# Attention probabilities and values as float32r parts with three products, values one token tile behind, the last heads under the next panel

## The chip, the cores and the metric

The kernel is one launch on one core of a Trainium2 chip. The metric is the device time of the launch in microseconds. Before the change it is 1859.57 us, the median of three runs (1858.75 to 1859.9).

## The reference, cut to what matters

Two transformer blocks over 512 tokens of width 1024, all in float32. Each has a windowed attention with 16 query heads of width 64 on 4 key and value heads. A block of 128 queries sees the key blocks beside it: three in the first block (before, own, after), two in the second (before, own), fewer at the ends of the sequence.

```
# first block (window_attention)
logits = jnp.where(valid, q @ k * 64 ** -0.5 + bias, -inf)
m = jnp.maximum(jnp.max(logits, -1), sink)
p = jnp.exp(logits - m)
p = p / (jnp.sum(p, -1) + jnp.exp(sink - m))
out = jnp.einsum('bngrqk,bnkgd->bnqgrd', p, vb)
# second block (swa_mixer): the same with ALiBi for a bias, divided after the product
o = jnp.einsum('bkgts,bskd->btkgd', p, vb) / denom
```

Around them stand projections, a state space branch, gates, norms and MLPs.

## The kernel before

Weights arrive as 66 panels of 1024 x 512, in eight steps (k) of 128 rows. For exact enough products in the float32r type, each operand is kept as a rounded part and a rest (`w_hi`, `w_lo`, `a_hi`, `a_lo`), and every product is three float32r matmuls: hi x hi, hi x lo, lo x hi. `main_step` does one step k of a panel: for each of four tiles m it waits, at k = 0, until DVE or ACT has freed that bank (`bank_free`), runs `before(m)`, then the three matmuls of 512 columns (L300), then `after(m)`. ACT rounds the weights (L259), GpSimd takes the rest (L263).

The attentions stand in four stretches of eight heads: `att1` (first block) and `att2` (second block), each for j = 0 and 1. In each, `query_panel` makes the queries (L1800 is its second half); then `heads` runs the next panel, one head behind another under its eight steps. Under step t, per token tile m: TensorE turns the probabilities of head t-1 (`pe_turn_p`, L789, 128x128 transposes into one PSUM bank, 2), the three panel matmuls, the values of head t-1 (`pe_values`, L802, float32, one product per key tile, into bank 3), the logits of head t+1 (`pe_logits`, L772 and L773, banks 0 and 1 in turn). A token tile has 2, 3, 3, 2 key tiles in `att1` and 1, 2, 2, 2 in `att2`. ACT copies the turned probabilities to SBUF (`act_turned`, L880) and takes the exponentials (`act_exp`, L850, from `lg` into `pr`); DVE adds bias and minimum to the logits (`dve_logits`, L819), sums and inverts the denominators (`dve_den`, L889, L891) and multiplies the output (`dve_out`, L897). `pe_values` of tile 0 waits for `dve_out` of the head before, as there is one values bank.

At the end of a stretch `att1` does head 7 on its own, after the panel. `att2` does it under the first step of the next panel (`last_head`). In both, DVE takes the panel's four banks one after another (L2162 with the gate bias, L2280 as a copy) and then does the denominators and output of head 7. In `att2` the gates (L2285, L2287) follow, and TensorE turns the gated outputs (L372) for the next operand.

The order on each engine is the program's order, written out by hand; semaphores tie the engines together. PE's loop over the heads before:

```
def before(m):
    if t: att.pe_turn_p(pe, j, t - 1, m)
def after(m):
    if t: att.pe_values(pe, j, t - 1, m)
    if t < 7: att.pe_logits(pe, j, t + 1, m, og)
main_step(pe, p + 1, t, h, l, False, og + 1, before=before, after=after)
```

## Time and profile before

| | us |
|---|---|
| median of three runs | 1859.57 |
| profiled execution | 1861.01 |
| its span | 1859.1 |
| TensorE matmul busy | 1810.3 (97%) |
| DVE busy | 832.6 (45%) |
| ACT busy | 848.2 (46%) |

The span is from the first to the last instruction of the profiled execution; its own time has 1.9 us around it. Times of rows are microseconds from the span's start, PE is a matmul on TensorE and PEld a weight load, which may run beside a matmul. A matmul's duration includes its way through the array, so what it costs in a queue is the distance between starts. L and a number is the line of the code; the name left of the arrow is written, those right of it are read. What stands in brackets behind an instruction is the idle time of its engine before it and what ended it. TensorE's granted clock is full in the stretches of the attentions.

### The profile page before, as it was taken

To read this page: it belongs to the slowest core of one execution; us is meant where nothing else is said; L and a number is where in the kernel's file an instruction comes from. 1 tells how busy PE (TensorE), PEld (TensorE's weight loads), DVE (VectorE), ACT (ScalarE), POOL (GpSimd) and SP (SyncE) were. 2 spreads that over 40 slices of the span, in tenths; PEclk is the share of its full clock that TensorE was granted. 3 is DMA by queue.
4 is the path that set the end of the run, shared out by engine and by line. 5 is a ranking of instruction groups with operands and counts; after the bars stand their busy time and mean duration, and the time that the engine had idled before them with its cause. 6 is when DMAs were issued, how large, how long until landed. Compare 5 with 4: busy or idle time off the path is not lost.

```text
span 1859.1 us, 26998 instructions
## 1 busy us (share of the span) xinstructions
PE 1810.3 (97%) x9064; PEld 1505.4 (81%) x9064; DVE 832.6 (45%) x1384; ACT 848.2 (46%) x1795; POOL 834.8 (45%) x598
## 2 busy tenths in 40 slices
PE   8999999999999999999999999999999999999998
PEld 7788888887888888888888888877888888887776
DVE  4688888888304443235430033050253311534644
ACT  4655555554325655324442244253533332456652
POOL 4654555577353132435444444445454444442322
PEclk9999999999999999999999999999999999999999
DMA  5732121222133121423233333324232223221211
GB/s 175 138 90 69 56 68 56 60 64 57 57 102 120 52 79 51 132 89 102 83 98 102 91 102 91 102 81 159 81 108 80 85 86 102 80 71 57 63 40 57
DMA packets 46223, 159.85 MB, mean 86 GB/s; under 512 B 4763, under 2 KB 7195, under 8 KB 45884
## 3 DMA queue, kind: packets, MB, share of 16 engines
q1 hardware_dynamic: 38592, 140.53, 24.7%
q10 hardware_dynamic: 7548, 18.20, 4.0%
q8 instruction: 54, 0.88, 0.2%
q14 instruction: 29, 0.24, 0.0%
HBM read 152.42 MB, written 6.29 MB: 85 GB/s over the span
## 4 chain that ended last, share of the span: by engine, by line
PE 81%; DVE 8%; issue 4%; ACT 4%; POOL 1%; DMA 1%; DVEq 0%; ACTq 0%; POOLq 0%
PE main L300 60%; PE main L328 4%; PE aux L802 4%; PE aux L656 2%; PE main L1800 2%; PE aux L789 2%; DVE u_acc L2002 1%; PE aux L772 1%; PE aux L372 1%; DVE x_res L564 1%; PE aux L773 1%; DVE y_all L2080 1%; PE aux L1888 1%; PE aux L647 1%; ACT w_hi L259 1%
## 5 line engine op out<-in xcount | busy, mean ns | idle before, releaser
L263 POOL TENSOR_TENSOR w_lo<-raw,w_hi 128x512 fp32r<-128x512 f32 x504 | 700.7, 1397 | 895.0 <-ACT w_hi L259 883.1
L259 ACT ACTIVATE w_hi<-raw 128x512 fp32r<-128x512 f32 x486 | 304.5, 630 | 696.7 <-PE main L300 683.7
L300 PE MATMUL main<-w_hi,a_hi 128*128 128x512 f32 x736 | 304.2, 413 | 2.3 <-ACT vv L1547 1.5
L300 PE MATMUL main<-w_hi,a_lo 128*128 128x512 f32 x736 | 288.1, 391 | 0.0
L300 PE MATMUL main<-w_lo,a_hi 128*128 128x512 f32 x736 | 287.3, 390 | 0.0
L300 PE MATMUL main<-a_hi,w_hi 128*128 128x512 f32 x576 | 231.2, 401 | 1.6 <-ACT u_raw L1296 1.6
L300 PE MATMUL main<-a_hi,w_lo 128*128 128x512 f32 x576 | 225.2, 391 | 0.0
L300 PE MATMUL main<-a_lo,w_hi 128*128 128x512 f32 x576 | 224.9, 390 | 0.0
L300 PEld LDWEIGHTS main<-w_hi,a_lo 128*128 128x128 f32 x736 | 138.1, 188 | 30.3
L300 PEld LDWEIGHTS main<-w_hi,a_hi 128*128 128x128 f32 x736 | 138.5, 188 | 28.4 <-ACT vv L1547 1.9
L300 PEld LDWEIGHTS main<-w_lo,a_hi 128*128 128x128 f32 x736 | 138.8, 189 | 23.0
L300 PE MATMUL main<-w_hi,f_hi 128*128 128x512 f32 x352 | 138.6, 394 | 1.5 <-DVE f_lo L385 1.5
L300 PE MATMUL main<-w_hi,f_lo 128*128 128x512 f32 x352 | 137.2, 390 | 0.0
L300 PE MATMUL main<-w_lo,f_hi 128*128 128x512 f32 x352 | 137.1, 389 | 0.0
L300 PEld LDWEIGHTS main<-a_hi,w_hi 128*128 128x128 f32 x576 | 108.5, 188 | 25.0 <-issue 2.8
L300 PEld LDWEIGHTS main<-a_hi,w_lo 128*128 128x128 f32 x576 | 108.4, 188 | 23.7
L300 PEld LDWEIGHTS main<-a_lo,w_hi 128*128 128x128 f32 x576 | 108.6, 188 | 22.3
L2002 DVE SCALAR_TENSOR_TENSOR u_acc<-u_raw,par,u_acc 128x510 f32<-128x510 f32 (+1 forms) x128 | 112.3, 946 | 2.4 <-DVE hst L2059 2.3
L802 PEld LDWEIGHTS aux<-v_sb,pt 128*128 128x128 f32 x544 | 70.3, 190 | 39.5 <-ACT pt L880 22.1
L802 PE MATMUL aux<-v_sb,pt 128*128 (+1 forms) x544 | 83.0, 278 | 4.5 <-ACT pt L880 2.9
L880 ACT ACTIVATE pt<-aux 128x256 f32<-128x256 f32 (+2 forms) x128 | 50.7, 397 | 75.5 <-PE aux L789 73.1
L300 PEld LDWEIGHTS main<-w_hi,f_hi 128*128 128x128 f32 x352 | 66.1, 188 | 15.1 <-DVE f_lo L385 1.8
(320 smaller groups left out, 3111.7 us busy)
## 6 DMA issues: line engine op xcount, KB each, us to landing
raw<-w_stream_in SPq DMA_DIRECT2D x264, 512.0 KB, 3.6
x_res<-x_in ACTq DMA_DIRECT2D x8, 512.0 KB, 5.1
rel_rows<-rel_row ACTq DMA_DIRECT2D x1, 4096.0 KB, 44.3
bias<-rel_rows ACTq DMA_DIRECT2D x2, 1536.0 KB, 8.3
out<-x_res SPq DMA_DIRECT2D x4, 512.0 KB, 2.7
bgate<-b_gate_in ACTq DMA_DIRECT2D x4, 256.0 KB, 5.8
ln_g<-ln_g_in ACTq DMA_DIRECT2D x1, 1024.0 KB, 4.7
ln_b<-ln_b_in ACTq DMA_DIRECT2D x1, 1024.0 KB, 6.8
```

The source lines that it names most:

```text
L259: eng.activation(w_hi[:, k, :], raw[:, k, :], ACT.Copy).then_inc(hi_done, 1)
L263: eng.tensor_tensor(w_lo[:, k, :], raw[:, k, :], w_hi[:, k, :].bitcast(F32), ALU.subtract).then_inc(lo_done, 1)
L300: mm = eng.matmul(mb[m][:, :], lhs, rhs, start=(first and k == 0 and n == 0), stop=(last and k == KT - 1 and n == 2))
L328: mm = eng.matmul(out, lhs, rhs, start=(first and k == 0 and n == 0), stop=(last and k == KT - 1 and n == 2))
L372: t = eng.transpose(b[:, m * P:m * P + P], self.src[:, m, c:c + P], ident)
L564: eng.scalar_tensor_tensor(x_res[:, m, :], self.fb[:, m, :], small[:, self.s + m:self.s + m + 1], x_res[:, m, :], ALU.mult, ALU.add).then_ ...
L656: x = eng.matmul(ab[c // 2][:, (c % 2) * GW + r * HP:(c % 2) * GW + r * HP + HP], dmat[r][:, dr, c * P:c * P + P], xdt[:, dr, c, r * HP:r ...
L789: x = eng.transpose(self.turned_bank(t, c)[:, b * P:b * P + P], self.pr[t % 2][:, c, off + b * P:off + b * P + P], ident)
L802: x = eng.matmul(ab[3][:, c * HP:c * HP + HP], pt[c % 2][:, b * P:b * P + P], v_sb[:, lo + b, bass.ds(j * P + half * HP, HP)], start=(b == ...
L880: eng.activation(pt[c % 2][:, 0:nb * P], self.turned_bank(t, c)[:, 0:nb * P], ACT.Copy).then_inc(p_in, 1)
L1800: mm = pe.matmul(mb[m][:, :], lhs, rhs, start=False, stop=(k == KT - 1 and n == 2))
L2002: ins = dve.scalar_tensor_tensor(acc, u_raw[:, m, i0:i0 + o1_ - o0], tap(m, k), acc, ALU.mult, ALU.add)
```

## The change

- Values: the turned value vectors go to `v_hl` as a rounded part (ACT) and a rest (DVE, new `dve_v`).
- Probabilities: ACT's copy of the turned probabilities becomes the rounded part `p_hi`; DVE subtracts it from the bank into `p_lo` (`dve_rest`, new). `pe_values` does three float32r products per key tile in place of one float32 product, with a wait for `p_rest` ahead of the last ones.
- The exponentials are written over the logits (`lg`), `pr` is gone. The four new tiles `pt` take its room.
- Turned probabilities use banks 1 and 2 in turn, logits bank 0 alone from the second head on.
- `pe_values` of a token tile comes one tile later; that of tile 3 under tile 0 of the next step. `dve_out` of a head comes one head later.
- Head 7 of both attentions runs under the first step (and the first tile of the second) of the next panel. DVE's taking of the four banks is now interleaved with `dve_rest` of that head. PE's loop over j in `att1` is written out.

The core of the diff:

```diff
-        v_sb = at("v_sb", R0 + 24 * KB, [P, NT, 256])
+        v_hl = at("v_hl", R0 + 20 * KB, [P, 4, NT, P], FR)
         lg = [at("lg0", B0 + 12 * KB, [P, NT, 384]), at("lg1", B0 + 24 * KB, [P, NT, 384])]
-        pr = [at("pr0", B0 + 18 * KB, [P, NT, 384]), at("pr1", B0 + 48 * KB, [P, NT, 384])]
-        pt = [at("pt0", R0 + 20 * KB, [P, 384]), at("pt1", R0 + 22 * KB, [P, 384])]
+        pt = [at(f"pt{i}", B0 + 18 * KB + 1536 * i, [P, 384], FR) for i in range(4)]
             def act_v(self, eng):
+                eng.wait_ge(v_turned, self.b + 2)
                 for j in range(2):
-                    eng.wait_ge(v_turned, self.b + j + 1)
-                    eng.activation(v_sb[:, :, j * P:j * P + P], ab[j][:, :].rearrange("p (c n) -> p c n", c=NT),
-                                   ACT.Copy).then_inc(v_in, 1)
+                    eng.activation(v_hl[:, 2 * j:2 * j + 2, :, 0:HP], self.turned_v(j), ACT.Copy).then_inc(v_hi, 1)
+
+            def dve_v(self, eng):
+                for j in range(2):
+                    eng.wait_ge(v_hi, self.b + j + 1)
+                    eng.tensor_tensor(v_hl[:, 2 * j:2 * j + 2, :, HP:P], self.turned_v(j),
+                                      v_hl[:, 2 * j:2 * j + 2, :, 0:HP].bitcast(F32), ALU.subtract).then_inc(v_in, 1)
...
-                if t == 0 and self.w == 384:
+                before = j * 32 + self.b * 32
+                if t > 0:
+                    eng.wait_ge(biased, one_up(n))
+                elif self.w == 384:
                     if c == 0:
-                        eng.wait_ge(biased, one_up(j * 32 + self.b * 32))
-                        eng.wait_ge(p_in, one_up(j * 32 + self.b * 32))
+                        eng.wait_ge(biased, one_up(before))
+                        eng.wait_ge(p_rest, one_up(before))
                         eng.wait_ge(att_out, one_up(j * 8 + self.b * 8))
-                elif c >= 2 or t > 0:
+                elif c >= 2:
                     eng.wait_ge(biased, one_up(n - 1))
                 else:
-                    eng.wait_ge(biased, one_up(j * 32 + self.b * 32))
+                    eng.wait_ge(biased, one_up(before))
+                    eng.wait_ge(p_rest, one_up(before))
...
             def logit_bank(self, t, c):
 
-                return ab[c if t == 0 and self.w == 384 else c % 2]
-
-            def turned_bank(self, t, c):
-
-                return ab[1 if t == 7 and c % 2 else 2]
+                if t == 0:
+                    return ab[c if self.w == 384 else c % 2]
+                return ab[0]
+
+            def turned_bank(self, c):
+
+                return ab[1 + c % 2]
 
             def pe_turn_p(self, eng, j, t, c):
                 n = j * 32 + (self.b * 32 + t * 4 + c)
                 lo, nb, off = self.span(c)
                 eng.wait_ge(exp_done, one_up(n + 1))
-                eng.wait_ge(p_in, one_up(n - 1 if t == 7 and c else n))
+                eng.wait_ge(p_rest, one_up(j * 32 + self.b * 32 if t == 0 and c < 2 else n - 1))
+                if t == 0 and c == 0:
+                    eng.wait_ge(biased, one_up(n + 4))
                 for b in range(nb):
-                    x = eng.transpose(self.turned_bank(t, c)[:, b * P:b * P + P], self.pr[t % 2][:, c, off + b * P:off + b * P + P], ident)
+                    x = eng.transpose(self.turned_bank(c)[:, b * P:b * P + P], self.lg[t % 2][:, c, off + b * P:off + b * P + P], ident)
                 x.then_inc(p_turned, 1)
...
                 for b in range(nb):
-                    x = eng.matmul(ab[3][:, c * HP:c * HP + HP], pt[c % 2][:, b * P:b * P + P],
-                                   v_sb[:, lo + b, bass.ds(j * P + half * HP, HP)],
-                                   start=(b == 0), stop=(b == nb - 1))
+                    for part in range(2):
+                        eng.matmul(out, self.p_hi[c % 2][:, b * P:b * P + P],
+                                   v_hl[:, head, lo + b, part * HP:part * HP + HP].rearrange("p o n -> p (o n)"),
+                                   start=(b == 0 and part == 0), stop=False)
+                eng.wait_ge(p_rest, one_up(n + 1))
+                for b in range(nb):
+                    x = eng.matmul(out, self.p_lo[c % 2][:, b * P:b * P + P],
+                                   v_hl[:, head, lo + b, 0:HP].rearrange("p o n -> p (o n)"), start=False, stop=(b == nb - 1))
                 x.then_inc(values, 1)
...
             def dve_logits(self, eng, j, t, cs=range(NT)):
                 for c in cs:
                     n = j * 32 + (self.b * 32 + t * 4 + c)
                     lo, nb, off = self.span(c)
                     eng.wait_ge(logits, one_up(n + 1))
-                    if c == 0:
-
-                        eng.wait_ge(exp_done, one_up(j * 32 + (self.b * 32 + max(t - 1, 0) * 4)))
-                        if t >= 2:
-                            eng.wait_ge(sink_exp, j * 8 + (self.b * 8 + t - 1))
+                    before = j * 32 + self.b * 32
+                    if t >= 2:
+                        eng.wait_ge(p_turned, before + (t - 2) * 4 + c + 1)
+                        eng.wait_ge(sink_exp, j * 8 + (self.b * 8 + t - 1))
+                    elif before:
+                        eng.wait_ge(p_turned, before)
...
             def act_heads(self, eng, j, p):
 
                 for t in range(8):
-                    if t:
-                        self.act_turned(eng, j, t - 1, [0, 1])
-                    self.act_exp(eng, j, t, [0, 1])
-                    if t:
-                        self.act_turned(eng, j, t - 1, [2])
-                    self.act_exp(eng, j, t, [2, 3])
-                    if t:
-                        self.act_turned(eng, j, t - 1, [3])
+                    for c in range(NT):
+                        if t:
+                            self.act_turned(eng, j, t - 1, [c])
+                        self.act_exp(eng, j, t, [c])
                     make_hi(eng, p, t)
                 self.act_turned(eng, j, 7)
...
-                    eng.activation(pt[c % 2][:, 0:nb * P], self.turned_bank(t, c)[:, 0:nb * P], ACT.Copy).then_inc(p_in, 1)
+                    eng.activation(self.p_hi[c % 2][:, 0:nb * P], self.turned_bank(c)[:, 0:nb * P], ACT.Copy).then_inc(p_in, 1)
+
+            def dve_rest(self, eng, j, t, c):
+
+                n = j * 32 + (self.b * 32 + t * 4 + c)
+                lo, nb, off = self.span(c)
+                eng.wait_ge(p_in, one_up(n + 1))
+                eng.tensor_tensor(self.p_lo[c % 2][:, 0:nb * P], self.turned_bank(c)[:, 0:nb * P],
+                                  self.p_hi[c % 2][:, 0:nb * P].bitcast(F32), ALU.subtract).then_inc(p_rest, 1)
...
             def dve_heads(self, eng, ch, j):
                 for t in range(8):
-                    if t:
-                        self.dve_den(eng, ch, j, t - 1)
-                    if t < 7:
-                        self.dve_logits(eng, j, t + 1)
-                    if t:
-                        self.dve_out(eng, j, t - 1)
+                    for c in range(NT):
+                        if t:
+                            self.dve_rest(eng, j, t - 1, c)
+                            if c == 0 and t >= 2:
+                                self.dve_out(eng, j, t - 2)
+                        if t < 7:
+                            self.dve_logits(eng, j, t + 1, [c])
+                        if t and c == 1:
+                            self.dve_den(eng, ch, j, t - 1)
+
+            def dve_last(self, eng, ch, j, c):
+
+                self.dve_rest(eng, j, 7, c)
+                if c == 0:
+                    self.dve_out(eng, j, 6)
+                    self.dve_den(eng, ch, j, 7)
...
                     def after(m):
-                        if t:
-                            att.pe_values(pe, j, t - 1, m)
+                        if t and m:
+                            att.pe_values(pe, j, t - 1, m - 1)
+                        elif t >= 2:
+                            att.pe_values(pe, j, t - 2, 3)
                         if t < 7:
                             att.pe_logits(pe, j, t + 1, m, og)
...
-            def attention(att, op, j, p, og):
-
-                query_panel(p, og, op, lambda m: first_logits(att, j, m, og))
-                heads(att, op, j, p, og)
-                att.pe_turn_p(pe, j, 7, 0)
-                for c in range(NT):
-                    if c < 3:
-                        att.pe_turn_p(pe, j, 7, c + 1)
-                    att.pe_values(pe, j, 7, c)
-
...
+            query_panel(P_QG, O_QG, ao, lambda m: first_logits(att1, 0, m, O_QG))
+            heads(att1, ao, 0, P_QG, O_QG)
+            query_panel(P_QG + 2, O_QG + 2, ao, lambda m: first_logits(att1, 1, m, O_QG + 2), last_head=last_of(att1, 0))
+            heads(att1, ao, 1, P_QG + 2, O_QG + 2)
+            before, after, later = last_of(att1, 1)
+            for k in range(KT):
+                if k == 0:
+                    main_step(pe, P_GA, k, *ao(k), False, O_GA, before=before, after=after)
+                elif k == 1:
+                    main_step(pe, P_GA, k, *ao(k), False, O_GA, after=lambda m: later() if m == 0 else None)
+                else:
+                    main_step(pe, P_GA, k, *ao(k), False, O_GA)
...
             for j in range(2):
                 att1.dve_take_k(dve, j)
                 dve.wait_ge(bias_landed, j * 16 + 16)
@@ -2160,7 +2224,7 @@
                 for m in range(NT):
                     wait_full(dve, j * 2 + (P_QG + 1), j * 2 + (O_QG + 1), m)
                     dve.tensor_tensor(gt[:, m, :], mb[m][:, :], bgate[:, :], ALU.add).then_inc(bank_free, 1)
-                att1.dve_den(dve, ch, j, 7)
+                    att1.dve_last(dve, ch, j, m)
                 att1.dve_out(dve, j, 7)
```

`last_of(att, j)` gives head 7's turning ahead of tile m, the values of the tile before behind it, and the values of tile 3 for the second step. In `att2` the same is done at the query panel of j = 1 and at the first output panel; `zt` is copied there with `att2.dve_last` behind each copy.

## Rows read from the trace of the kernel before

**Rows 1.** The page: busy times, and the chain that ended last by engine.
```profile
PE 1810.3 (97%) x9064; PEld 1505.4 (81%) x9064; DVE 832.6 (45%) x1384; ACT 848.2 (46%) x1795; POOL 834.8 (45%) x598
PE 81%; DVE 8%; issue 4%; ACT 4%; POOL 1%; DMA 1%; DVEq 0%; ACTq 0%; POOLq 0%
```

**Rows 2.** Chain that ended last, one head apart: start, length, what.
```profile
591.18 0.76 PE aux L802 x6
...
599.08 0.76 PE aux L802 x6
```

**Rows 3.** Timeline, one token tile of att1: start, length, instruction, idle before.
```profile
600.65 0.19 PEld L300 LDWEIGHTS main<-w_hi,a_lo 128*128 128x128 f32 x1
600.88 0.40 PE L300 MATMUL main<-w_hi,a_lo 128*128 128x512 f32 x1
601.16 0.74 PEld L802 LDWEIGHTS aux<-v_sb,pt 128*128 128x128 f32 x6 [0.32 <-ACT pt L880]
...
601.82 0.19 PEld L772 LDWEIGHTS aux<-k_hh,q_hl 128*128 128x128 f32 x1
```

**Rows 4.** The page, costliest groups: busy, mean ns, idle before.
```profile
L802 PE MATMUL aux<-v_sb,pt 128*128 (+1 forms) x544 | 83.0, 278 | 4.5 <-ACT pt L880 2.9
```

**Rows 5.** Timeline, first head's logits in att2, j = 1, one key tile.
```profile
1752.09 0.19 PEld L772 LDWEIGHTS aux<-k_hh,q_hl 128*128 128x128 f32 x1
1752.32 0.22 PE L772 MATMUL aux<-k_hh,q_hl 128*128 128x128 f32 x1
1752.32 0.19 PEld L773 LDWEIGHTS aux<-k_ll,q_hl 128*128 128x128 f32 x1
1752.37 0.28 PE L773 MATMUL aux<-k_ll,q_hl 128*128 128x128 f32 x1
1752.43 0.19 PEld L300 LDWEIGHTS main<-w_hi,a_hi 128*128 128x128 f32 x1
```

**Rows 6.** Who waited for whom, weight loads: us in total, times, longest.
```profile
PEld aux L802 <- ACT pt L880: 22.1, 90, 0.3
PEld aux L802 <- DVE o L897: 11.9, 24, 0.6
PEld aux L802 <- issue: 5.5, 8, 1.9
```

**Rows 7.** Timeline, end of att2's first stretch, start of the next panel.
```profile
1721.50 0.42 DVE L897 TENSOR_TENSOR o<-aux,small 128x256 f32<-128x256 f32 x1 [4.03 <-PE aux L802]
1721.96 2.48 DVE L2280 COPY zt<-main 128x512 f32<-128x512 f32 x4
...
1722.75 0.30 PE L789 MATMUL aux<-const,pr2b 128*128 128x128 f32 x1 [1.36 <-issue]
...
1723.76 0.39 PE L789 MATMUL aux<-const,pr2b 128*128 128x128 f32 x2
...
1724.18 0.38 ACT L880 ACTIVATE pt<-aux 128x256 f32<-128x256 f32 x1 [0.81 <-PE aux L789]
...
1724.36 0.15 DVE L889 TENSOR_TENSOR small<-small 128x4 f32<-128x4 f32 x1
...
1724.55 0.18 DVE L891 RECIPROCAL small<-small 128x4 f32<-128x4 f32 x1
```

**Rows 8.** Busy time by engine, first stretch of att1: us, then each engine's.
```profile
583.15:646.00 62.85, 61.96 (x394) 50.20 (x392) 25.95 (x85) 40.74 (x119) 14.93 (x12) 1.00 0.16 45
```

**Rows 9.** Timeline, the first head of att1: second logits, DVE's first, third logits.
```profile
584.99 0.34 PE L772 MATMUL aux<-k_hh,q_hl 128*128 128x384 f32 x1
...
585.83 0.48 DVE L819 CUSTOM_DVE_ANT_0 lg<-aux,bias,ssq 128x256 f32<-128x256 f32 x1
...
586.38 0.45 PE L772 MATMUL aux<-k_hh,q_hl 128*128 128x384 f32 x1 [0.19 <-DVE small L819]
```

**Rows 10.** Timeline, TensorE turning the gated outputs of att2, both stretches.
```profile
1741.53 0.33 PE L372 MATMUL aux<-const,o 128*128 128x128 f32 x1 [1.66 <-DVE o_lo L385]
...
1814.19 0.33 PE L372 MATMUL aux<-const,o 128*128 128x128 f32 x1 [1.46 <-DVE o L2287]
```

More of the change, by code:

```diff
@@ L795, in pe_values, with pe_last_before, pe_last_after, after @@
                 lo, nb, off = self.span(c)
+                if t == 0 and c == 0:
+                    eng.wait_ge(v_in, self.b + 2)
                 if c == 0:
-                    if t == 0:
-                        eng.wait_ge(v_in, self.b + 2)
                     eng.wait_ge(att_out, one_up(j * 8 + (self.b * 8 + t)))
                 eng.wait_ge(p_in, one_up(n + 1))
+                head = bass.ds(j * 2 + half, 1)
+                out = ab[3][:, c * HP:c * HP + HP]
                 for b in range(nb):
-                    x = eng.matmul(ab[3][:, c * HP:c * HP + HP], pt[c % 2][:, b * P:b * P + P],
-                                   v_sb[:, lo + b, bass.ds(j * P + half * HP, HP)],
-                                   start=(b == 0), stop=(b == nb - 1))
-                x.then_inc(values, 1)
+                    for part in range(2):
[6 more added lines that the diff above has]
+                                   v_hl[:, head, lo + b, 0:HP].rearrange("p o n -> p (o n)"), start=False, stop=(b == nb - 1))
+                x.then_inc(values, 1)
+            def pe_last_before(self, eng, j):
+                return lambda m: self.pe_turn_p(eng, j, 7, m)
+            def pe_last_after(self, eng, j):
+                def after(m):
+                    if m:
+                        self.pe_values(eng, j, 7, m - 1)
+                    else:
+                        self.pe_values(eng, j, 6, 3)
+                return after
             def dve_logits(self, eng, j, t, cs=range(NT)):
@@ L845, in act_exp @@
                     eng.wait_ge(den_done, one_up(j * 8 + (self.b * 8 + max(t - 1, 0))))
-                    eng.wait_ge(values, one_up(j * 32 + (self.b * 32 + max(t - 1, 0) * 4)))
                 for c in cs:
@@ L849, in act_exp @@
                     eng.wait_ge(biased, one_up(j * 32 + (self.b * 32 + t * 4 + c + 1)))
[L850 removed]
+                    eng.activation(self.lg[t % 2][:, c, off:off + nb * P], self.lg[t % 2][:, c, off:off + nb * P], ACT.Exp,
                                    bias=small[:, ng + c:ng + c + 1], scale=-1.0,
@@ L885, in dve_den @@
                 sm, es = small[:, 36 + 4 * (t % 2):40 + 4 * (t % 2)], small[:, 44 + 4 * (t % 2):48 + 4 * (t % 2)]
-                dn, rc = small[:, 52:56], small[:, 56:60]
+                dn, rc = small[:, 52:56], small[:, self.per_den(t):self.per_den(t) + 4]
                 eng.wait_ge(sink_exp, q + 1)
@@ L1149, in _ @@
                 load_quarter(sp, 0, q)
-            for semaphore in (logits, biased, values, exp_done, den_done, p_in, att_out, f_ready, sp_y, yt_turned, yt_ready, z_gate, sp_full):
+            for semaphore in (logits, biased, values, exp_done, den_done, p_in, p_rest, att_out, f_ready, sp_y, yt_turned, yt_ready, z_gate, sp_full):
                 sp.sem_inc(semaphore, 1)
@@ L1789, in query_panel @@
                         main_step(pe, p, k, h, l, True, og, before=last_head[0], after=last_head[1])
+                    elif k == 1 and last_head is not None:
+                        main_step(pe, p, k, h, l, True, og, after=lambda m: last_head[2]() if m == 0 else None)
                     else:
@@ L1824, in first_logits, with last_of @@
                     att.pe_logits(pe, j, 0, c, og)
-            def attention(att, op, j, p, og):
-                query_panel(p, og, op, lambda m: first_logits(att, j, m, og))
-                heads(att, op, j, p, og)
-                att.pe_turn_p(pe, j, 7, 0)
-                for c in range(NT):
-                    if c < 3:
-                        att.pe_turn_p(pe, j, 7, c + 1)
-                    att.pe_values(pe, j, 7, c)
-            with pe.Fori(0, 2) as j:
-                attention(att1, ao, j, j * 2 + P_QG, j * 2 + O_QG)
-            panel(P_GA, O_GA, ao, False)
+            def last_of(att, j):
+                return att.pe_last_before(pe, j), att.pe_last_after(pe, j), lambda: att.pe_values(pe, j, 7, 3)
+            query_panel(P_QG, O_QG, ao, lambda m: first_logits(att1, 0, m, O_QG))
[8 more added lines that the diff above has]
+                    main_step(pe, P_GA, k, *ao(k), False, O_GA, after=lambda m: later() if m == 0 else None)
+                else:
+                    main_step(pe, P_GA, k, *ao(k), False, O_GA)
             pe.wait_ge(att_out, one_up(NQ))
@@ L1936, in _ @@
                 if k == 0:
-                    main_step(pe, P_BO, k, *o_at(k), False, O_BO, before=lambda m: att2.pe_turn_p(pe, 1, 7, m),
-                              after=lambda m: att2.pe_values(pe, 1, 7, m))
+                    main_step(pe, P_BO, k, *o_at(k), False, O_BO, before=before2, after=after2)
+                elif k == 1:
+                    main_step(pe, P_BO, k, *o_at(k), False, O_BO, after=lambda m: later2() if m == 0 else None)
                 else:
```

32 lines of the change are left out of this document (19 added, 13 removed).

## The prediction

> **What bounds the kernel now.** I read the page first. TensorE is busy for 97% of the span and carries 81% of the chain that ended last; DVE and ACT are at 45% and 46% [rows 1]. So the question is what TensorE's queue gets more or less of. The change lies in four stretches of eight heads each, in which one attention's small matmuls stand between the matmuls of a large panel: two of the first attention (about 584 to 646 us and 669 to 732 us) and two of the second (about 1671 to 1728 us and 1752 to 1807 us). In the chain a head of the first attention repeats after 7.90 us [rows 2]: TensorE sets the pace, and a small wait in each token tile comes on top.
>
> How large that wait is can be read where one token tile is laid out [rows 3]. The third main matmul starts at 600.88. The first weight load of the values could start right with it, but starts at 601.16, when ACT has copied the turned probabilities. The next group's weights load at 601.82: six loads took 0.66 us, 0.11 us each. A free queue would have put the second load at the main matmul's end (600.88 + 0.23 = 601.11) and the group behind at 601.11 + 5 x 0.11 = 601.66. So of a late start of 0.28 us, 0.12 us are covered and 0.16 us reach TensorE's time.
>
> **The values, three products for two instructions.** The float32 values are 544 matmuls and 544 weight loads for 272 pairs of 128x128 probabilities and 128x64 values: two instructions per pair [rows 4]. The change makes them three float32r products per pair, each with its own weight load: 816 instructions, 272 more. What does one cost? Float32r matmuls of 128 columns are seen in the first logits of the second attention [rows 5]. Their weight loads start at 1752.32 and 1752.43, 0.11 us apart. The matmuls start only 0.05 us apart (1752.32, 1752.37), but the second lasts 0.28 us where the first lasts 0.22: the 0.06 us more are its wait for its weights. So 0.11 us pass from one to the next, and with 64 columns there is still less to stream: the weight load decides, at 0.108 to 0.11 us. That is what the float32 instructions cost too (0.11 us, [rows 3]). The rounded form is thus not cheaper per instruction, and there are half as many again: 272 x 0.108 = +29.4 us. Nothing hides it, as it is TensorE's own queue. Bounds: 0.05 us per instruction, if the starts of those two matmuls [rows 5] are taken as they stand (816 x 0.05 - 544 x 0.108 = -18 us), and 0.127 us, the six value instructions with their wait in the chain (0.76 us / 6, [rows 2]; 816 x 0.127 - 58.8 = +45 us). I take 0.108, since both weight loads that I can compare, of float32 and of float32r, give it.
>
> The rule of the Trainium skill that speaks against my figure is in "TensorE: Matmul & The Clock Gate", section "Weight-path perf modes": the fast weight load is on with 128 weights and a type other than FP32, which read literally takes float32r in. An estimate by its factor of two would be 816 x 0.054 - 58.8 = -14.7 us instead of +29.4 us. The same table says that 4-byte weights win nothing, and section "LDWEIGHTS (loading the stationary operand)" gives columns / 1.2 ns, 107 ns; by these the term is 272 x 0.107 = +29 us, and the spacing of 0.11 us in the trace agrees with them.
>
> **Values one token tile behind.** This removes TensorE's waits before the values: 90 of 22.1 us for ACT's copy, 24 of 11.9 us for the output that frees the values' bank, 8 of 5.5 us counted as issue [rows 6]. These are idle times of the weight loads; of each, 0.04 us are there without any wait (600.84, the end of the load before, to 600.88) and 0.12 us are covered, as worked out above. 39.5 - 122 x 0.16 = 20.0 us reach TensorE. All of it should go: in the new order a copy (0.38 us for two key tiles, [rows 7]; about 0.5 for three) and the new subtraction on DVE (an estimate: 0.42 us for two key tiles as the output multiply of that size, 0.55 for three, [rows 7]) have a whole token tile of about 2 us behind the turning. I take -20.0 us. If the wait for the output stayed, 24 x (0.50 - 0.16) = 8 us of it would stay: bounds -12 and -20.
>
> DVE gets the 128 subtractions of about 0.5 us, some 2 us per head of about 8.3 us in which it has 3.2 us of other work (25.95 us in a stretch of eight, [rows 8]): it is not the bound. ACT does the same work as before, 5.1 us per head. The exponentials written over the logits, the value tiles split in two (two subtractions per attention, while the query panel runs) and the unrolled loop cost nothing: TensorE works for more than 20 us on the query panel in between.
>
> **One logits bank.** From the second head on the logits have one bank instead of two, so each tile's logits wait for DVE to have read the tile before. In the steady state the DVE step is done about 0.8 us into a token tile, and TensorE comes back after 2 us: nothing. In the first head it costs: DVE is busy with the queries until 585.83, takes the first logits until 586.31, and the second logits, issued at 584.99 before, must wait for that; then the pace is restored. Third logits come at about 587.5 instead of 586.38 [rows 9]: +1.1 us, about 1 us in each of the four stretches, +4 us (bounds 0 and 6).
>
> **Last heads under the next panel.** In the second attention this is so already; the first attention ran the last head alone, and its work is the same under a panel. What changes in all four places is DVE's order. Main banks must be freed before the next panel's first step, and TensorE waits for each bank ahead of turning that tile. DVE used to free all four in one go, 2.48 us, 0.62 us each [rows 7]. Now between two of them stands the subtraction of the last head, and that waits for TensorE's turning and ACT's copy. Bank to bank it is then: 0.42 us from the start of the turning to the copy, 0.38 us of copy, 0.42 us of subtraction, 0.62 us of freeing, about 0.1 us of signals, 1.95 us [rows 7], against TensorE's work in the second attention of two turnings, three main matmuls of 0.23 us and six products: 0.22 + 0.70 + 0.66 = 1.58 us. Between the first and the second bank DVE also has to wait for the values of the head before (1.47 us into the tile, + 0.1), then multiply out (0.42), the sum and reciprocal (0.4, [rows 7]) and free (0.62): 3.1 us, against 1.47. I lay the four out: 0.5 + 1.6 + 0.7 (only one key tile in the tile behind) + 0.4 = 3.2 us of wait, against 1.36 us in the present order [rows 7]. In the first attention, with three key tiles, 0.1 + 1.6 + 0.6 + 0.2 = 2.5 us; its present waits are in the 20.0 us above. So 2 x 2.5 + 2 x (3.2 - 1.36) = +8.7 us. In the second attention the last output multiply is what the gates, and then TensorE's turning of the outputs, hang on: TensorE already idles 1.66 and 1.46 us there for DVE [rows 10]. The multiply comes 3.8 us later, the queue 3.3 to 3.4 us: +0.4 us each, +0.8 us. Together +9.5 us (bounds 0 and 14).
>
> **Sum.** 29.4 - 20.0 + 4.0 + 9.5 = +22.9 us. The profiled execution took 1861.0 us (span 1859.1 and 1.9 around it), so 1883.9; the median of the runs is 1.4 us under it: 1882.5, I say 1883.
>
> **The rivals.** (a) Rounded weight loads at half the time, or the second product with the same rounded probabilities using the weights that lie there already. The first, at the half of 0.108 us, gives -14.7 - 20 + 13.5 = -21 us, 1839 us: this is the case on the other side, and it decides from the price of one product under 0.108 - 22.9 / 816 = 0.080 us. Against it speak the 0.11 us spacing, and that the logits load the same queries twice, for both key parts [rows 5]. If the reload alone fell, with about 0.03 us left of that instruction, 272 x 0.078 = 21 us go and the time is 1862. The fast weight load of the Trainium skill ("TensorE: Matmul & The Clock Gate", "Weight-path perf modes") would be such a case. Chance 5% for both. (b) The bank waits don't come, because DVE reaches each bank in time: 22.9 - 13.5 = +9.4 us, 1869 us. For it: my estimate stands on a chain of small durations. Against: the 1.36 us that the simple order already costs [rows 7]. 12%. (c) A new wait in every token tile, on the single logits bank or on DVE's subtraction: the place is the logits step; it needs DVE to be over 1 us later than laid out. 0.2 us in 112 tiles is +22 us, 1905 us. 10%. (d) Products above 0.108 us, for the wait that now stands between the rounded ones and the rest: at 0.119 us 9 us more, 1892 us; it counts to the forecast, which gets 73%.
>
> **How the numbers follow.** The forecast with its own bounds is 1875 to 1895. Case (b) lies on its lower side and half of (c) on its upper, so 1868 to 1900 leaves out (a) and much of (c), near 15%. A measurement of this kernel tells about 0.2% (3.7 us) from no change. Faster takes half or more of (a), 4%; the same 2%; slower 94%.
>
> **What would show it.** After: 816 value matmuls, 0.11 us apart; heads of the first attention at 7.90 less about 0.7 (20.0 us over 28 heads) plus 10 x 0.108, about 8.3 us, hardly any wait of value weight loads for ACT or the output; idle of TensorE of about 1.6 us ahead of the second bank at the four ends, released by DVE's freeing of the bank. Wrong would be the whole if value matmuls stood 0.06 us apart, or if heads got shorter than 7.9 us; the term of the ends, if the first step of the next panels ran without a gap.

## The result, and the profile after

The changed kernel takes 1902.22 us (median of 4 runs, 1901.81 to 1904.39) where the kernel before takes 1859.16 us beside it (4 runs, 1858.30 to 1859.90): ratio 1.0234, 95% interval 1.0216 to 1.0252. It is slower, as forecast, but by 43 us and not by 23: 1902 lies above the range of 1868 to 1900.

The head of the page of the kernel after, with busy times and the chain by engine, answers to [rows 1]:

```profile
span 1900.0 us, 27607 instructions
PE 1847.4 (97%) x9336; PEld 1559.3 (82%) x9336; DVE 882.5 (46%) x1516; ACT 846.1 (45%) x1795; POOL 834.5 (44%) x598
PE 82%; DVE 8%; issue 4%; ACT 3%; POOL 1%; DMA 1%; DVEq 0%; ACTq 0%; POOLq 0%
```

272 more matmuls (9336 less 9064), 37 us more of TensorE's busy time and 41 us more of span: still a kernel that TensorE bounds.

One head apart in the chain of the kernel after (start, length, what), where [rows 2] had 7.90 us:

```profile
601.11 0.33 PE aux L806 x3
601.44 0.69 PE main L299 x3
602.14 0.59 PE aux L822 x6
602.73 0.34 PE aux L827 x3
...
609.52 0.33 PE aux L806 x3
609.85 0.70 PE main L299 x3
610.54 0.59 PE aux L822 x6
611.13 0.34 PE aux L827 x3
```

A head repeats after 609.52 - 601.11 = 8.41 us; forecast was about 8.3. The nine products of three key tiles take 0.59 + 0.34 = 0.93 us, 0.103 us each.

The steady state is thus as forecast. The ends are not. This is the timeline of the kernel after where the next panel's first step begins, first stretch of att1 (start, length, instruction, idle before it); of the kernel before, [rows 7] shows such an end:

```profile
648.98 0.69 DVE L2226 TENSOR_TENSOR gt<-main,bgate 128x512 f32<-128x512 f32 x1 [0.25 <-DVE small L936]
649.73 0.55 PE L806 MATMUL aux<-const,lg 128*128 128x128 f32 x3 [1.75 <-DVE gt L2226]
650.03 0.48 PE L299 MATMUL main<-a_hi,w_hi 128*128 128x512 f32 x1
650.35 0.40 PE L299 MATMUL main<-a_lo,w_hi 128*128 128x512 f32 x1
650.58 0.40 PE L299 MATMUL main<-a_hi,w_lo 128*128 128x512 f32 x1
...
652.05 0.90 PE L806 MATMUL aux<-const,lg 128*128 128x128 f32 x3 [0.48 <-DVE gt L2226]
652.60 0.78 PE L299 MATMUL main<-a_hi,w_hi 128*128 128x512 f32 x1
653.17 0.63 PE L299 MATMUL main<-a_lo,w_hi 128*128 128x512 f32 x1
653.60 0.63 PE L299 MATMUL main<-a_hi,w_lo 128*128 128x512 f32 x1
654.03 1.32 PE L822 MATMUL aux<-v_hl,pt 128*128 128x64 f32 x6
655.09 0.76 PEld L827 LDWEIGHTS aux<-v_hl,pt 128*128 128x128 f32 x3
655.16 0.83 PE L827 MATMUL aux<-v_hl,pt 128*128 128x64 f32 x3
```

TensorE waits 1.75 us for the second bank, near the 1.6 laid out, and 0.48 us for the third. Then something else starts: the main matmuls at 653.17 and 653.60 stand 0.43 us apart, those at 650.35 and 650.58 stand 0.23 us apart. The same instructions take nearly twice as long. Busy time in windows around this end and around that of att1's second stretch, of the kernel after (us, then busy time and count of PE, PEld, DVE, ACT and POOL, the granted clock, DMA share, GB/s):

```profile
640.00:652.00 12.00, 9.82 (x71) 8.87 (x69) 6.13 (x15) 5.03 (x15) 1.61 (x2) 0.99 0.14 44
652.00:668.00 16.00, 15.95 (x58) 13.86 (x59) 7.28 (x10) 6.61 (x12) 2.67 (x2) 0.58 0.35 116
668.00:684.00 16.00, 16.00 (x75) 13.42 (x74) 9.22 (x17) 6.84 (x12) 3.98 (x5) 1.00 0.20 66
736.00:750.00 14.00, 12.47 (x91) 11.51 (x91) 6.77 (x19) 6.68 (x22) 2.58 (x2) 1.00 0.09 30
750.00:766.00 16.00, 15.83 (x61) 13.80 (x60) 5.83 (x10) 4.59 (x9) 1.30 (x2) 0.57 0.07 25
```

For 16 us behind the waits the granted clock averages 0.58 and 0.57, which is the lower level (1.2 GHz, half of 2.4) for most of the time; TensorE is busy throughout and gets 58 matmuls through where the next 16 us hold 75. The same happens at the ends of att2, briefly at the first, for long at the second. The windows there:

```profile
1750.00:1756.00 6.00, 4.77 (x22) 4.20 (x23) 3.06 (x8) 0.77 (x2) 0.00 (x0) 0.72 0.26 87
1756.00:1762.00 6.00, 6.00 (x34) 5.16 (x33) 3.61 (x7) 5.80 (x11) 0.14 (x1) 1.00 0.02 4
1826.00:1834.00 8.00, 7.69 (x55) 6.96 (x54) 4.17 (x13) 5.55 (x19) 1.28 (x1) 1.00 0.01 2
1834.00:1854.00 20.00, 18.47 (x65) 15.78 (x66) 9.72 (x19) 4.03 (x10) 2.56 (x2) 0.57 0.07 27
```

(1 - 0.58) x 16 + (1 - 0.57) x 16 + (1 - 0.72) x 6 + (1 - 0.57) x 20 = 24 us of TensorE's work at full clock are lost there by the granted clock. Not all of it is time of the kernel: some of it lies inside TensorE's waits, and some takes the place of waits for DVE further on. In the profiled execution of the kernel before the clock is full at all four ends.

The waits of the kernel after, weight loads (us in total, times, longest), answer to [rows 6]:

```profile
PEld aux L785 <- DVE small L857: 9.2, 12, 1.7
PEld aux L806 <- DVE gt L2226: 4.4, 4, 1.9
PEld aux L806 <- DVE zt L2345: 3.5, 3, 1.6
```

No weight load of the values (L822, L827) waits for ACT's copy or for the output any more: the 39.5 us of [rows 6] are gone. What has grown are the waits of the first heads' logits on the single bank (L785; 2.1 us in the kernel before), and new are the turnings of the last heads on the main banks that DVE frees (L806).

To see the parts I cut each profiled execution at the same events of its timeline. Stretch 1 of an attention runs from the first matmul of the second half of its query panel (L1856 in the kernel after, L1800 in the one before) to the same matmul of the next panel. Stretch 2 runs from there to TensorE's first turning of the outputs (att1) or to its last turning of the gated outputs (att2), so the last heads under the next panel lie within. Times in us:

| kernel | before att1 | att1, 1 | att1, 2 | between | att2, 1 | att2, 2 | end | span |
|---|---|---|---|---|---|---|---|---|
| before | 571.2 | 85.8 | 99.4 | 902.8 | 77.7 | 77.3 | 44.9 | 1859.1 |
| after | 571.2 | 99.9 | 113.0 | 900.4 | 83.9 | 86.8 | 44.8 | 1900.0 |
| e1 | 571.0 | 91.2 | 104.7 | 900.3 | 80.5 | 79.7 | 44.8 | 1872.3 |
| e2 | 571.7 | 94.3 | 107.6 | 899.9 | 83.5 | 82.5 | 44.9 | 1884.3 |
| c1 | 570.8 | 80.6 | 94.1 | 898.8 | 74.2 | 71.8 | 46.5 | 1836.8 |
| c2 | 571.3 | 82.0 | 95.6 | 899.9 | 74.2 | 73.0 | 46.5 | 1842.5 |

Outside the four stretches nothing was changed, and the executions still differ by up to 4 us there (898.8 to 902.8), where single stretches of a lower clock fall in one and not in another. So a step between two kernels is good to some 3 us.

### The profile page after: what moved, and what is told of

The parts are those of the page before. It is cut to its first block, busy times and chain, and to the rows that moved or that the text cites. A ratio compares the mean times of both kernels' runs of the same rounds, so it can differ in the third digit from the quotient of the medians.

```text
span 1900.0 us, 27607 instructions
## 1 busy us (share of the span) xinstructions
PE 1847.4 (97%) x9336; PEld 1559.3 (82%) x9336; DVE 882.5 (46%) x1516; ACT 846.1 (45%) x1795; POOL 834.5 (44%) x598
## 4 chain that ended last, share of the span: by engine, by line
PE 82%; DVE 8%; issue 4%; ACT 3%; POOL 1%; DMA 1%; DVEq 0%; ACTq 0%; POOLq 0%
PE main L299 60%; PE main L327 4%; PE aux L822 3%; PE aux L806 2%; PE aux L655 2%; PE main L1856 2%; PE aux L827 2%; DVE u_acc L2065 1%; PE aux L785 1%; PE aux L371 1%; DVE x_res L563 1%; PE aux L786 1%; DVE y_all L2143 1%; PE aux L1949 1%; PE aux L646 1%
## 5 line engine op out<-in xcount | busy, mean ns | idle before, releaser
L299 PEld LDWEIGHTS main<-w_lo,a_hi 128*128 128x128 f32 x736 | 139.6, 190 | 22.9
L913 ACT ACTIVATE pt<-aux 128x256 fp32r<-128x256 f32 (+2 forms) x128 | 51.0, 398 | 116.8 <-PE aux L806 114.8
L822 PEld LDWEIGHTS aux<-v_hl,pt 128*128 128x128 f32 x544 | 86.1, 203 | 12.6
L299 PEld LDWEIGHTS main<-w_hi,f_lo 128*128 128x128 f32 x352 | 66.1, 188 | 14.0
```

What stands on the lines that cost most here:

```text
L299: mm = eng.matmul(mb[m][:, :], lhs, rhs, start=(first and k == 0 and n == 0), stop=(last and k == KT - 1 and n == 2))
L822: eng.matmul(out, self.p_hi[c % 2][:, b * P:b * P + P], v_hl[:, head, lo + b, part * HP:part * HP + HP].rearrange("p o n -> p (o n)"), sta ...
L913: eng.activation(self.p_hi[c % 2][:, 0:nb * P], self.turned_bank(c)[:, 0:nb * P], ACT.Copy).then_inc(p_in, 1)
```

## The experiments

Two theories stood for the 20 us too many. A: the waits at the four ends are as sized, and what was left out is the clock that falls behind them. B: the products cost more than 0.108 us each, or another of the four terms was mis-sized, and the lower clock is a companion. The runs take the change apart into its four terms.

**e1: the banks freed in one go.** At both kinds of ends DVE again frees all four main banks first and does the last head's subtractions and outputs behind that; all else as in the kernel after.

```
 for m in range(NT):
     ...
     dve.tensor_tensor(gt[:, m, :], mb[m][:, :], bgate[:, :], ALU.add).then_inc(bank_free, 1)
+for m in range(NT):
     att1.dve_last(dve, ch, j, m)
```

(The same at the end of att2, with its copy to zt.)

> The changed kernel with one thing undone: at the four ends of the stretches DVE frees all four main banks in one go, and only then takes the rests, the output and the denominators of the last heads. Theory A (the interleaved order makes TensorE wait 1.5 to 1.75 us for the second bank, and behind these waits its granted clock falls to the lower level for some 7 to 17 us): the waits shrink by about 2.4 us at each end (-9.6 us) and the clock stays up behind all four ends (about -20 us), 1870 to 1876 us. Theory B (the low clock after the ends comes from something else in the change): only the waits go, 1892 us, and the low clock at 652 to 667, 752 to 765 and 1837 to 1853 us stays.

Measured: 1875.82 us (4 runs, 1873.96 to 1878.10), 1.0099 [1.0078, 1.0121] against the kernel before: 26.4 us less than the kernel after. The timeline of e1 at the same end (no idle time stands behind TensorE's instructions), and busy time in windows around it, with the full clock:

```profile
645.34 2.47 DVE L2226 TENSOR_TENSOR gt<-main,bgate 128x512 f32<-128x512 f32 x4
...
646.12 0.41 PE L806 MATMUL aux<-const,lg 128*128 128x128 f32 x2
646.28 0.48 PE L299 MATMUL main<-a_hi,w_hi 128*128 128x512 f32 x1
```

```profile
640.00:652.00 12.00, 12.00 (x90) 11.14 (x89) 6.82 (x17) 5.56 (x17) 1.44 (x2) 1.00 0.15 46
652.00:668.00 16.00, 16.00 (x80) 13.52 (x80) 11.73 (x12) 8.46 (x16) 6.34 (x4) 1.00 0.56 180
```

26.4 us are more than both the term of the ends (9.5) and its upper bound (14). One order of DVE's work at four places carries them. This does not yet tell waits from clock.

**e2: the waits filled.** The kernel after, with matmuls of 512 columns that nobody reads put into TensorE's queue ahead of each bank wait: 7, 3 and 2 of them, 48 in all. DVE's order and the banks are those of the kernel after, so TensorE can't get on any earlier; it only isn't idle.

```
+if fill is not None:
+    fill(m)            # m = 1, 2, 3: 7, 3, 2 matmuls of 512 columns
 if first and k == 0 and free_wait:
     eng.wait_ge(bank_free, (og - 1) * 4 + m + 1)
```

> The changed kernel with DVE's interleaved order kept, so the banks come as late as before, but with twelve added matmuls of 512 columns at each end (7, 3 and 2 ahead of the waits for the second, third and fourth bank), whose results nobody reads. Theory A (idle of TensorE ahead of the banks brings the clock down): the added 48 matmuls lie in the waits, the clock stays up, and the kernel with more work is faster, 1880 to 1886 us. Theory B (the clock falls for another reason, or the waits alone cost the time): 1902 us or a few more.

Measured: 1885.70 us (4 runs, 1883.79 to 1886.90), 1.0147 [1.0127, 1.0167]. The kernel does more than the one after and is 16.5 us faster. Its timeline at the first end, and the window behind it:

```profile
648.30 1.86 PE L1893 MATMUL aux<-a_hi 128*128 128x512 f32 x7
649.46 0.69 DVE L2238 TENSOR_TENSOR gt<-main,bgate 128x512 f32<-128x512 f32 x1 [0.26 <-DVE small L938]
650.20 0.55 PE L808 MATMUL aux<-const,lg 128*128 128x128 f32 x3
...
653.21 0.39 PE L301 MATMUL main<-a_lo,w_hi 128*128 128x512 f32 x1
653.44 0.40 PE L301 MATMUL main<-a_hi,w_lo 128*128 128x512 f32 x1
```

```profile
652.00:668.00 16.00, 16.00 (x87) 13.60 (x87) 11.27 (x13) 7.78 (x14) 6.20 (x4) 1.00 0.45 148
```

DVE begins to free the second bank at 649.46 and has done at 650.15, and TensorE gets on at 650.20. That is 0.5 us later than in the kernel after, but so is the turning ahead of the first bank (646.77 for 646.29), which comes before any filler: here the filler fits into the wait. At the third and the fourth bank it is a little too long. DVE is done with them at 652.47 and 654.86, and TensorE's turning starts at 652.65 and 655.14, some 0.3 us of delay in all. But the main matmuls behind stay 0.23 us apart, the clock is 1.00, and 16 us hold 87 matmuls for 58. This separates the two shares of the 26.4 us: 1902.2 - 1885.7 = 16.5 us are the clock, 1885.7 - 1875.8 = 9.9 us are the waits, with the little that the filler adds to them (about 1 us at the four ends together, an estimate from e2's timeline there). The 24 us of lost clock above are more than 16.5 because the low clock hides waits: e2 idles 1.91 us for DVE ahead of turning the last gated outputs (1839.44), where the kernel after has no wait any more (1855.20).

By stretch, after less e2 is 5.6, 5.4, 0.4 and 4.3 us; e2 less e1 is 3.1, 2.9, 3.0 and 2.8 us. The waits, filled by the same 12 matmuls everywhere, cost nearly the same at each end. The clock doesn't: at the third end it was back after some 3.4 us.

**b1: late banks in the kernel before.** The kernel before, with no other part of the change; at both ends of att2 DVE repeats the copies that free the second, third and fourth bank (4, 2 and 1 times more).

```
+for again in range({1: 4, 2: 2, 3: 1}.get(m, 0)):
+    ch(dve.tensor_copy(zt[:, m, :], mb[m][:, :]))
 dve.tensor_copy(zt[:, m, :], mb[m][:, :]).then_inc(bank_free, 1)
```

> The kernel before, in which DVE repeats its copies at the two ends of the second attention (four times for the second bank, twice for the third, once for the fourth), so that TensorE waits about 1.9 and 0.6 us for banks there; nothing else is changed. By the waits alone: +2.5 to 3 us at each end, 1864 to 1865 us. By theory A (such waits bring the granted clock down behind them): up to 7 us more at each end, less what lies in TensorE's wait for DVE's gates, 1868 to 1876 us, with a low clock at about 1728 and 1808 us.

Measured: 1868.61 us (4 runs, 1866.86 to 1869.83), 1.0055 [1.0033, 1.0076] against 1857.31 beside it. The timeline at the first of the two ends, and two windows, from inside the wait on:

```profile
1725.52 0.69 PE L789 MATMUL aux<-const,pr2b 128*128 128x128 f32 x2 [2.28 <-DVE zt L2282]
1725.86 0.78 PE L300 MATMUL main<-a_hi,w_hi 128*128 128x512 f32 x1
1726.43 0.63 PE L300 MATMUL main<-a_lo,w_hi 128*128 128x512 f32 x1
1726.86 0.63 PE L300 MATMUL main<-a_hi,w_lo 128*128 128x512 f32 x1
```

```profile
1724.00:1732.00 8.00, 6.48 (x28) 5.66 (x28) 4.91 (x10) 1.71 (x5) 0.00 (x0) 0.58 0.14 54
1732.00:1740.00 8.00, 8.00 (x37) 6.62 (x37) 7.57 (x10) 5.72 (x10) 3.25 (x2) 1.00 0.00 0
```

With a wait of 2.28 us, in a kernel without any rounded value product, the clock falls (0.43 us from matmul to matmul, 0.58 in the window), and at the second end too (0.50 over 1810 to 1812). The wait doesn't stand alone: 3.5 us before its end stands one of 1.36 us for the first bank (1722.06). The kernel before has that first wait as well [rows 7], and the full clock. So the lower clock needs none of the new products; late banks can bring it. The time lies in the 1868 to 1876 us of theory A, above the 1864 to 1865 of the waits alone. The 11 us hold both parts. The second turning starts 3.46 us behind the first (1722.06 to 1725.52) for 1.01 in the kernel before [rows 7], which is 2.45 us of waiting at each end; the stretches are 4.8 and 3.9 us longer.

**c1: the float32 kernel with the order of the change.** The kernel before, with its float32 values, but each token tile's values one tile behind, the last head of all four stretches under the next panel, and the banks freed in one go. This is the change without the three products, the single bank, the exponentials written over the logits, and the broken order of DVE at the ends.

```
-if t:
-    att.pe_values(pe, j, t - 1, m)
+if t and m:
+    att.pe_values(pe, j, t - 1, m - 1)
+elif t >= 2:
+    att.pe_values(pe, j, t - 2, 3)
```

(DVE's outputs and logits follow: the output of tile 3 after the next head's first turning; last_of for the panels as in the change.)

> The kernel before (float32 values in two instructions, exponentials in their own tile, two logits banks) with one part of the change alone: values one token tile behind, last heads of all four stretches under the next panel, all banks freed in one go. If the 39.5 us of idle of the value weight loads hold 20.0 us of TensorE's time, as predicted: 1859 - 20 - about 1 = 1838 us. If the waits come back elsewhere (the output multiply, which now comes one head later): above 1850 us.

Measured: 1838.52 us (4 runs, 1838.40 to 1838.75), 0.9895 [0.9877, 0.9912]: 20.3 us less than the kernel before, and the fastest kernel of this study. Its waits, weight loads:

```profile
PEld aux L372 <- DVE o L2302: 4.4, 2, 2.6
...
PEld aux L789 <- issue: 1.9, 3, 1.5
```

None of the values (L802) is left. Most of the last line is one wait in the first head of att2 (1.36 us ahead of the turning at 1662.71), where the kernel before waits 1.52 us. A head takes 7.30 us in its chain (597.95 to 605.25) where it took 7.90 [rows 2]. At the second end of att2 the turning of the gated outputs waits 2.13 us for DVE in c1's timeline (weight loads at both ends together 4.4 us), where it waited 1.46 us [rows 10]: with DVE's last outputs behind the banks, part of the gain is given back there. And behind this wait the clock falls as well:

```profile
1790.31 1.09 PE L372 MATMUL aux<-const,o 128*128 128x128 f32 x8 [2.13 <-DVE o L2302]
```

```profile
1790.00:1796.00 6.00, 5.69 (x24) 4.73 (x25) 1.54 (x3) 2.12 (x4) 2.51 (x2) 0.72 0.01 3
```

(1 - 0.72) x 6 = 1.7 us of work are lost there. That is why the stage behind att2 takes 46.5 us in c1 for 44.9 in the kernel before; c2 has the same wait (2.15 us) and the same 46.5 us, e1 waits 1.93 us there, keeps the full clock and takes 44.8.

**c2: one logits bank.** c1 with a single bank from the second head on.

```
-return ab[c if t == 0 and self.w == 384 else c % 2]
+return ab[(c if self.w == 384 else c % 2) if t == 0 else 0]
 ...
+elif t > 0:
+    eng.wait_ge(biased, one_up(n))
 elif c >= 2:
     eng.wait_ge(biased, one_up(n - 1))
```

> The kernel of c1_float32_one_behind with the logits of the second and later heads in one bank, as in the changed kernel. My prediction prices this at about 1 us in each stretch (the first head, while DVE takes the queries), +4 us, 1842 to 1843 us. If the single bank also holds up every token tile, +0.1 us in each of 112 tiles or more: 1854 us and above.

Measured: 1844.19 us (4 runs, 1843.71 to 1846.79), 0.9928 [0.9907, 0.9950]: 5.7 us more than c1. By stretch it is 1.4, 1.5, 0.0 and 1.2 us, together 4.1; the rest lies outside the attentions. The 0.0 hides a cost: c2 has the first head's waits there too (0.94 us at 1663.33), and in exchange c1's 1.36 us wait of the same head is gone. In the kernel after, the place is seen directly (weight loads of the second, third and fourth logits, each with its wait for DVE; compare [rows 9]):

```profile
586.31 0.19 PEld L785 LDWEIGHTS aux<-k_hh,q_hl 128*128 128x128 f32 x1 [1.67 <-DVE small L857]
587.65 0.19 PEld L785 LDWEIGHTS aux<-k_hh,q_hl 128*128 128x128 f32 x1 [0.46 <-DVE small L857]
588.99 0.19 PEld L785 LDWEIGHTS aux<-k_hh,q_hl 128*128 128x128 f32 x1 [0.46 <-DVE small L857]
```

**e3, e5 and e6: what a product costs.** e3 is the kernel after with two products per pair, e5 is e1 with two, e6 is e1 with four (the product of the two rests added).

```
-for part in range(2):
+for part in range(1):
```

> The changed kernel without the product of the rounded probabilities with the rest of the values, which is left out of the computation: 272 matmuls and weight loads fewer. At 0.108 us each and with nothing else in the way: -29.4 us, 1873 us, as my prediction priced them. If a product with 64 columns that repeats the weights of the one before costs less than the others: less than that.

Measured: 1866.12 us (8 runs, 1859.78 to 1871.54), 1.0043 [1.0027, 1.0060]: 36.1 us less than the kernel after where 29.4 were expected, 0.133 us a product. But in its profiled execution the granted clock is low at three of the ends and full at that of att1's second stretch, where the kernel after has 0.57, and its runs scatter by 12 us. This is no clean price, so it was measured again without the waits:

> The kernel of e1_banks_first without the product of rounded probabilities and rest of the values (left out of the computation), 272 matmuls with their weight loads fewer. With the clock up behind the ends in both, the difference to e1_banks_first is the price of the products alone: at 0.108 us each -29.4 us, 1846 us. If the instruction that repeats its neighbour's weights were cheaper: less than -20 us.

Measured: 1844.29 us (4 runs, 1843.69 to 1845.36), 0.9924 [0.9904, 0.9944].

> The kernel of e1_banks_first with a fourth product, rest of the probabilities with rest of the values: 272 matmuls more. At 0.108 us each +29.4 us, 1905 us. A straight line through two, three and four products says that TensorE's queue has no slack in the stretches; a smaller step from two to three than from three to four would mean that something else had hidden part of the third.

Measured: 1903.68 us (4 runs, 1900.54 to 1903.78), 1.0239 [1.0217, 1.0262]. From e5 over e1 to e6 the steps are 31.5 and 27.9 us, (1903.68 - 1844.29) / 544 = 0.109 us a product. e5 and e6 ran beside the same runs of the kernel before and e1 beside others. Set against the kernel before beside each, the steps are 30.0 and 29.4 us, nearly a straight line: nothing hid part of the third product.

## Why the forecast was wrong, point by point

The runs make a chain from the kernel before to the one after, in which each step is one term of the sum. The waits of 1.36 us at att2's two ends that the order of c1 takes away (2.7 us) stand with the first step, and come back in the last:

| step | forecast | measured |
|---|---|---|
| before to c1: values one behind, -20.0; ends of att2, -2.7 | -22.7 | -20.3 |
| c1 to c2: one logits bank | +4.0 | +5.7 |
| c2 to e1: three products | +29.4 | +31.6 |
| e1 to after: DVE's order at the ends, 9.5 + 2.7 | +12.2 | +26.4 |
| together | +22.9 | +43.4 |

(Each step is a difference of medians. c2, e5, e6 and b1 ran on another chip than c1, e1, e2 and e3; the kernel before took 1857.3 us beside the first and 1858.9 us beside the second group. Set against it, c1 to c2 is 7.2 us and c2 to e1 30.1 us, so these two steps are good to about 1.5 us. Beside the kernel after, the kernel before took 1859.2 us, so that the whole is 43.1 us there. c2 to e1 also holds the subtractions and the exponentials written over the logits.)

**The step that failed** is the last one. As the prediction put it, "Together +9.5 us (bounds 0 and 14)". Its waits were right: 3.1, 2.9, 3.0 and 2.8 us at the four ends (e2 less e1) for 2.5, 2.5, 3.2 and 3.2, 11.8 us with the filler's share, and 9.9 us by the medians, for 12.2. (Its sum for the second bank was off by a little: 1.47 + 0.1 + 0.42 + 0.4 + 0.62 is 3.0 and not 3.1 us, so 1.5 us of wait; the kernel after shows 1.75, 1.53, 1.53 and 1.53.) What stood in no term is what TensorE does after them: 16.5 us more, because its clock falls to 1.2 GHz and stays there, at three of the four ends for 10 us or more, mostly in matmuls of the next panel, which the change doesn't touch. With those 16.5 us the forecast of 1883 would have been 1899.5. The prediction asked of a stall only what it costs while it lasts. None of the rivals had it either; the only one of about the same time, (c), a new wait in every token tile at 1905 us, was not what happened, as no such wait is in the rows.

**Right: the products.** 0.109 us each by e5 and e6, 0.11 us by heads (8.41 less 7.30 us between after and c1 is 1.11 us for ten products), for 0.108; rival (d), 0.119 us, is not borne out by them. The bounds of 0.05 and 0.127 us are out, and so is rival (a): the rounded form is not cheaper per instruction. By stretch, e1 less c2 is 9.2 and 9.1 us in att1 (80 products each) and 6.3 and 6.7 in att2 (56 each), 0.11 to 0.12 us each. The estimate from the fast weight load of the Trainium skill ("TensorE: Matmul & The Clock Gate", section "Weight-path perf modes — Fast Weight Load (FWL) and DoubleRow"), -14.7 us, is refuted by e5 and e6; the figure of its section "LDWEIGHTS (loading the stationary operand)" is borne out by them.

**Right: values one tile behind.** A head of att1 is 0.60 us shorter (7.90 to 7.30) for some 0.7 us forecast, and all value waits are gone; of the waits in the first heads one of 1.36 us on ACT stays, ahead of a turning. By stretch c1 is 5.2, 5.3, 3.5 and 5.5 us under the kernel before, 19.5 in all; by medians it gives 20.3 us for 22.7. Of the 2.4 us missing, 1.6 are in the stage behind att2 (44.9 to 46.5 us), where the clock falls behind the wait of 2.13 us: the term that the prediction left out shows in the float32 kernel too.

**Nearly right: one logits bank.** The waits are where they were laid out, ahead of the second and third logits, and the third come at 587.65 where 587.5 was forecast. But the fourth waits 0.46 us as well: the pace is not restored after the third. In three stretches it costs 1.2 to 1.5 us, in the fourth c1's own wait is gone for it; together 4.1 us, by medians 5.7.

**Wrong in its weight: rival (b)**, that the bank waits don't come. They come at all four ends.

**The Trainium skill** has a place that bears on this and that the prediction doesn't draw on: "TensorE: Matmul & The Clock Gate", section "A second HAM failure mode: psum-queue depth-cycling", tells of a kernel whose short idle times between groups of matmuls, repeated in every iteration, let the clock go down and up, and puts the loss to that. The rows at 649.73 and behind, and e2, agree with it in kind: 9.9 us of waiting bring a loss of 16.5 us of clock. Here it takes no repetition through the kernel: one end with a wait or two is enough.

**Still open**: what decides whether the clock falls, and for how long. In the kernel after the wait for the third bank can have had a part at the first end alone: there the clock falls inside that wait (0.90 over 651 to 652, 0.50 over 652 to 653), at the second before it begins (0.90 over 750 to 751, the wait of 0.17 us ends at 751.74), and at the two ends of att2 inside the wait for the second bank (0.95 over 1750 to 1751, 0.62 over 1836 to 1837). But waits of this size don't always bring it. At att1's second end e3 has waits of 1.52, 0.72 and 0.49 us and the full clock (1.00 over 728 to 740), and the waits of 1.66 and 1.46 us of [rows 10] and e1's 1.93 us leave it full as well, where 2.13 us in c1 don't. It stays down for some 3.4 us at the third end, 14 us at the first two and 17 us at the last, and no run shows why.

## What to carry to other kernels

Where TensorE is the bound, price a new wait twice: once for itself, and once for the matmuls behind it at half clock, if the clock falls. Here that was 1.7 times as much again for waits of 1.5 to 1.8 us. It didn't fall behind every wait of that size, so it belongs into the range, and the granted clock behind each wait has to be looked at. Free all banks first and put an engine's long chains behind that: the place of one call inside or behind a loop, at four ends, was worth 26 us. And take a change apart before judging it: of four parts here, the one that pays (values one tile behind, -20 us) is independent of the one that costs (three products for two instructions, +30 us), and c1 keeps only the first.

## What the runs showed of the hardware that I had not expected

- A wait of 1.75 us and one of 0.48 us, with three turnings, three main matmuls and six products between them, come with the granted clock's lower level for some 14 us (0.58 over 652 to 668; it falls inside the second wait), though TensorE is 99.7% busy in them (15.95 of 16 us).
- 48 matmuls that compute nothing make a kernel 16.5 us faster (1902.2 to 1885.7 us).
- A wait of 1.53 us, with one of 0.31 us 3 us before it, can be enough (the clock falls inside it, at about 1750.9), and one of 1.93 us can leave the clock full (e1, at 1827.45).
- At the lower level the weight loads slow down with the matmuls: six products take 1.13 us (654.03 to 655.16) for 0.59 us in the steady state, and three weight loads 0.76 us (655.09) for 0.41 us (645.80, the same line at full clock).
- A product of 64 columns costs 0.109 us with rounded float32 operands, as much as each of the two instructions of a float32 product [rows 3].
